# Last down phase of a decoder layer: tokens 0 to 256 as the stationary operand, four weight tiles as the moving one

## What is computed

```python
x = layer_norm(ALPHA * x + merged @ w_out, ln1_g, ln1_b)
f = (jax.nn.silu(x @ w_ff_gate) * (x @ w_ff_up)) @ w_ff_down
x = layer_norm(ALPHA * x + f, ln2_g, ln2_b)
```

## Time and profile before

| | us |
|---|---|
| median of 3 runs | 929.28 (929.07 to 929.48) |
| the profiled execution | 929.93 |
| its span in the trace | 927.1 |

### The profile page before, as it was taken

How to read it: one execution, slowest core, us unless ns; L and a number is a source line. 1 busy time by engine, 2 the same in 40 slices (tenths; PEclk the granted TensorE clock), 3 DMA queues, 4 the chain that set the end, 5 groups by cost and what they waited for, 6 DMA issues and landing times.

```text
span 927.1 us, 18700 instructions
## 1 busy us (share of the span) xinstructions
PE 911.2 (98%) x7211; PEld 906.1 (98%) x7211; DVE 769.3 (83%) x1147; ACT 453.2 (49%) x783; POOL 328.8 (35%) x330
## 2 busy tenths in 40 slices
PE   9999999999999999999999999999999999999995
PEld 8999999999999999999999999999999999999995
DVE  2699999999869888877786699988888888788456
ACT  4422232226666634555543457676546656455432
POOL 4666565758300000000005451455633546321104
PEclk9999999999999999999999999999999999999998
DMA  7733333222436534332334230533443333432412
GB/s 228 200 86 92 89 100 90 71 66 80 139 120 227 183 95 122 97 108 80 107 97 136 70 91 1 138 92 92 121 108 92 92 92 98 129 93 63 133 34 96
DMA packets 169813, 98.49 MB, mean 106 GB/s; under 512 B 5338, under 2 KB 165890, under 8 KB 169745
## 3 DMA queue, kind: packets, MB, share of 16 engines
q1 hardware_dynamic: 167513, 96.66, 35.9%
q10 hardware_dynamic: 2232, 0.92, 0.4%
HBM read 89.94 MB, written 7.62 MB: 105 GB/s over the span
## 4 chain that ended last, share of the span: by engine, by line
PE 89%; DVE 5%; POOL 2%; ACT 2%; issue 1%; DMA 1%; SPq 0%; POOLq 0%; DVEq 0%; ACTq 0%
PE main L1550 38%; PE main L1711 33%; PE aux L1711 5%; PE main L1783 3%; PE aux L1550 3%; PE main L2046 1%; PE aux L1536 1%; PE aux L1963 1%; POOL h_f L886 1%; PE main L1963 1%; DMA raw<-in_w_in 1%; PE main L1586 1%; POOL r_tok L937 1%; POOL r_tok L939 0%; DVE aux L2563 0%
## 5 line engine op out<-in xcount | busy, mean ns | idle before, releaser
L757 POOL TENSOR_TENSOR w_lo<-raw,w_hi 128x1024 fp32r<-128x1024 f32 (+1 forms) x46 | 110.3, 2403 | 343.1 <-ACT w_hi L949 336.2
L1550 PE MATMUL main<-x_hi,w_lo 128*128 128x272 f32 x752 | 156.0, 288 | 0.0
L1550 PE MATMUL main<-x_hi,w_hi 128*128 128x272 f32 x752 | 155.7, 289 | 0.0
L1550 PE MATMUL main<-x_lo,w_hi 128*128 128x272 f32 x752 | 155.2, 288 | 0.0
L949 ACT ACTIVATE w_hi<-raw 128x1024 fp32r<-128x1024 f32 x103 | 108.6, 1057 | 70.3 <-PE main L1550 38.0
L1550 PEld LDWEIGHTS main<-x_lo,w_hi 128*128 128x128 f32 x752 | 118.2, 189 | 0.0
L1550 PEld LDWEIGHTS main<-x_hi,w_lo 128*128 128x128 f32 x752 | 118.1, 188 | 0.0
L1550 PEld LDWEIGHTS main<-x_hi,w_hi 128*128 128x128 f32 x752 | 117.4, 189 | 0.0
L2171 DVE SCALAR_TENSOR_TENSOR aux<-glu_pad,miscT,aux 128x512 f32<-128x512 f32 x112 | 75.1, 747 | 0.0
L894 POOL TENSOR_TENSOR h_lo<-h_f,h_hi 128x272 fp32r<-128x272 f32 x50 | 49.3, 992 | 56.4 <-ACT h_hi L1383 55.5
L1550 PE MATMUL main<-y,w_hi 128*128 128x272 f32 x384 | 63.6, 288 | 0.0
(11 more groups left out here) (467 smaller groups left out, 2927.1 us busy)
## 6 DMA issues: line engine op xcount, KB each, us to landing
raw<-in_w_in SPq DMA_DIRECT2D x63, 512.0 KB, 4.1
raw<-in_w_ff_gate SPq DMA_DIRECT2D x22, 512.0 KB, 4.0
raw<-in_w_ff_up SPq DMA_DIRECT2D x22, 512.0 KB, 5.3
raw<-in_w_branch SPq DMA_DIRECT2D x32, 256.0 KB, 3.5
raw<-in_w_ff_down SPq DMA_DIRECT2D x32, 256.0 KB, 3.9
raw<-in_w_out SPq DMA_DIRECT2D x8, 512.0 KB, 3.9
raw<-in_w_ff_down SPq DMA_DIRECT2D x16, 192.0 KB, 3.4
kept_sums<-g_made_hi SPq DMA_DIRECT2D x4, 544.0 KB, 3.6
```

The source lines that it names most:

```text
L757: pool.tensor_tensor(w_lo[s][:, 0:n, :], raw[s][:, 0:n, :], w_hi[s][:, 0:n, :].bitcast(F32), ALU.subtract).then_inc(w_lo_ready, 1)
L1550: mm = pe.matmul(ps[:, h, :], w[s][:, k, :], x[:, h * HALF:(h + 1) * HALF], start=(first and k == 0 and j == 0), stop=(last and k == n - 1 ...
```

## The change

The eight tiles are done in the order 0, 2, 1, 3, 4, 6, 5, 7, for columns 256 to 544 alone (`item_a`, weights stationary as before, 288 columns moving). Tokens 0 to 256 are done after all of these in four pieces (`item_b`): the hidden rows of 128 tokens are stationary, and four weight tiles, 512 columns, move. Sums come out by rows: partition = token. So all eight weight tiles are kept split until the end (`rows_w`, in the places of `w_hi`, `w_lo`, `x_hi` and `x_lo`). What must still be turned for these tokens is `merged` as it was before the third phase (`turn_b`); ACT copies it to `r_tok` (`rows_b`), DVE adds the sums there (`add_b`) and measures 512 columns at once (`measure_b`). POOL's part of the last norm is reduced to group 3 and to 256 columns of group 1.

```diff
-         + [("ff", q) for q in range(15, KF - 2)] + [("plain", m) for m in range(KD)])
+         + [("ff", q) for q in range(15, KF - 2)] + [("plain", m) for m in (0, 2, 1, 3, 4, 6, 5, 7)])
+TURNS = (("a", 0), ("a", 1), ("a", 2), ("a", 3), ("r", 0), ("a", 4), ("r", 1), ("a", 5), ("r", 2),
+         ("a", 6), ("a", 7), ("r", 3))
...
+            def item_a(i, f):
+
+                for k, (wt, x) in enumerate(plain_weights(S_PLAIN + i, f)):
+                    mm = pe.matmul(a_bank(i), wt, x[:, C_A:NT],
+                                   start=(f == f0 and k == 0), stop=(f == KF - 1 and k == 2))
...
+            def item_b(t, f):
+
+                j, h = divmod(t, 2)
+                k = f // 2 - FIRST_PAIR[2] + f % 2 * PAIRS[2]
+                wh, wl = (rows_w[h][b][:, :, k, :] for b in range(2))
+                xh, xl = (x[:, j * P:j * P + P] for x in hid_row(f))
+                out = b_bank(t).rearrange("p (m n) -> p m n", m=RING)
+                for n, (wt, x) in enumerate(((wl, xh), (wh, xl), (wh, xh))):
+                    mm = pe.matmul(out, x, wt, start=(f == f0 and n == 0), stop=(f == KF - 1 and n == 2))
...
+            def turn_b(t):
...
+                for m in range(RING):
+                    mm = pe.transpose(main[:, 1 + 2 * h, m * P:m * P + P],
+                                      merged[:, RING * h + m, j * P:j * P + P], ident[:, :])
...
+            def add_b(t):
+
+                j, c = t // 2, t % 2 * RING * P
+                rows_ = r_tok[:, j, c:c + RING * P]
+                ve.wait_ge(plain_done, KD + t + 1)
+                ve.wait_ge(rows_out, turned_at("r", t))
+                ve.tensor_tensor(rows_, b_bank(t), rows_, ALU.add).then_inc(plain_out, 1)
+
+            def measure_b(t):
+
+                j, c = t // 2, t % 2 * RING * P
+                ve.wait_ge(plain_out, KD + t + 1)
+                link(ve.bn_stats(bn[:, j, t % 2, :], r_tok[:, j, c:c + RING * P]))
...
-            for n, (j, cols) in enumerate(((3, slice(0, D)), (2, slice(D // 2, D)), (1, slice(D // 2, 3 * D // 4)),
-                                           (1, slice(3 * D // 4, D)))):
+            for n, (j, cols) in enumerate(((3, slice(0, D)), (1, slice(3 * D // 4, D)))):
```

More of the change, by code:

```diff
@@ L1476, in last_rows @@
[L1476 to L1485, removed]
+            left_high(s + 5)
@@ L1957, in plain_weights @@
                 return (wl[:, k, :], xh), (wh[:, k, :], xl), (wh[:, k, :], xh)
[L1959 to L1964, removed]
-                return mm
[L1967 to L1972, removed]
+            f0 = 2 * FIRST_PAIR[2]
@@ L1999, in _ @@
                 for f in range(f0, f0 + 4):
-                    plain(m, f, first=(f == f0))
-                if m == 0:
+                    item_a(i, f)
+                if i == 0:
                     product_4(S_PLAIN - 1)
-            for m in range(2):
+            for i in range(RING):
                 pe.wait_ge(hid_lo_ready, made(lo_order, 2, 2, "a21"))
-                plain(m, f0 + 4)
+                item_a(i, f0 + 4)
                 pe.wait_ge(hid_lo_ready, made(lo_order, 2, 2, "a22"))
-                plain(m, f0 + 5, last=True).then_inc(plain_done, 1)
@@ L2008, in _ @@
-            for m in range(2, WHOLE):
-                pe.wait_ge(left_lo_ready, S_PLAIN + m + 1)
-                pe.wait_ge(plain_out, m - 1)
+                item_a(i, f0 + 5).then_inc(plain_done, 1)
+            for i in range(RING, KD):
+                pe.wait_ge(left_lo_ready, S_PLAIN + i + 1)
+                pe.wait_ge(plain_out, i - 3)
+                for f in range(f0, f0 + 4):
+                    item_a(i, f)
+                if i == 4:
+                    turn_a(0)
+                    turn_a(1)
+                elif i == 5:
+                    turn_a(2)
+                    turn_a(3)
+                    turn_b(0)
+                else:
+                    turn_a(i - 2)
+                    turn_b(i - 5)
+                item_a(i, f0 + 4)
+                item_a(i, f0 + 5).then_inc(plain_done, 1)
@@ L2011, in _ @@
+            pe.wait_ge(plain_out, 5)
+            for f in range(f0, f0 + 4):
+                item_b(0, f)
+            turn_a(6)
+            turn_a(7)
+            turn_b(3)
+            item_b(0, f0 + 4)
+            item_b(0, f0 + 5).then_inc(plain_done, 1)
+            for t in range(1, 4):
+                if t == 3:
+                    pe.wait_ge(rows_out, turned_at("r", 3))
+                else:
+                    pe.wait_ge(plain_out, (6, 8)[t - 1])
                 for f in range(f0, KF):
-                    if f == f0 + 4:
-                        for before in ((0, 1) if m == 2 else (m - 1,)):
-                            turn_rows(before)
@@ L2015, in _ @@
-                    mm = plain(m, f, first=(f == f0), last=(f == KF - 1))
+                    mm = item_b(t, f)
                 mm.then_inc(plain_done, 1)
[L2018 to L2029, removed]
@@ L2049, in _ @@
-            turn_last(len(LAST) - 1)
         @block.vector
@@ L2826, in last_statistics, with measure_a @@
+            def measure_a(i):
+                ve.wait_ge(rows_turned, turned_at("a", i))
+                for j in range(3):
+                    q = P if j < 2 else B * T
+                    ins = ve.bn_stats(bn[0:q, 2 + j, M_ORDER[i], :], aux[0:q, i % 2, j * P:j * P + P])
+                    if j < 2:
                         link(ins)
                 ins.then_inc(rows_measured, 1)
+            def add_b(t):
[4 more added lines that the diff above has]
+                ve.tensor_tensor(rows_, b_bank(t), rows_, ALU.add).then_inc(plain_out, 1)
@@ L2860, in finish @@
                   .then_inc(rows_ready, 1)
-            left, right = slice(0, D // 2), slice(D // 2, D)
+            whole = slice(0, D)
             s = S_PLAIN
@@ L2891, in _ @@
+            measure_a(5)
+            add_a(7)
+            measure_a(6)
+            measure_a(7)
             aggregate(0)
-            add_last(4)
+            ve.wait_ge(bn_var, 1)
+            ve.wait_ge(vecs_copied, 2)
+            ve.wait_ge(rows_out, turned_at("a", 7))
+            weigh(rs_tok[:, :], B * T, NTILE, whole)
             last_scale(0)
-            ve.wait_ge(vecs_copied, 2)
-            ve.wait_ge(rows_out, WHOLE + 4)
-            weigh(rs_tok[:, :], B * T, NTILE, slice(0, D))
@@ L2907, in _ @@
+            finish(r_tok[:, 2, :], P, 2, whole)
+            add_b(1)
+            measure_b(1)
             aggregate(1)
             ve.wait_ge(bn_var, 2)
-            ve.wait_ge(rows_out, WHOLE + 8)
-            weigh(r_tok[:, 0, left], P, 0, left)
+            weigh(r_tok[:, 0, :], P, 0, whole)
             last_scale(1)
-            weigh(r_tok[:, 0, right], P, 0, right)
-            finish(r_tok[:, 0, :], P, 0, slice(0, D))
+            finish(r_tok[:, 0, :], P, 0, whole)
+            add_b(2)
@@ L2914, in _ @@
+            measure_b(2)
+            add_b(3)
+            measure_b(3)
+            aggregate(2)
+            ve.wait_ge(bn_var, 3)
+            left, third = slice(0, D // 2), slice(D // 2, 3 * D // 4)
             weigh(r_tok[:, 1, left], P, 1, left)
-            for cols in (slice(0, D // 4), slice(D // 4, D // 2)):
-                finish(r_tok[:, 1, cols], P, 1, cols)
+            last_scale(2)
+            finish(r_tok[:, 1, left], P, 1, left)
+            weigh(r_tok[:, 1, third], P, 1, third)
@@ L2919 @@
+            finish(r_tok[:, 1, third], P, 1, third)
 N_SMALL = 21
```

265 lines of the change are left out of this document (123 added, 142 removed).

## The result

| | before | changed |
|---|---|---|
| median, us | 929.38 (929.07 to 929.48, 4 runs) | 924.02 (923.39 to 924.67, 4 runs) |
| the profiled execution | 929.93 | 924.05 |
| its span | 927.1 | 922.1 |

The ratio is 0.9941, with a 95% interval of 0.9928 to 0.9953. The change makes the kernel faster by 5.4 us. 3.6 were forecast, so the direction is right, and the time lies at the lower edge of the range (as ratios, 0.9941 against 923.9 / 929.28 = 0.9942).

What follows compares the result with a forecast made beforehand. POOL's share of the last norm was taken to set the old end, DVE's list the new: 903.6 plus 14.4 gives 918.0, the tail 921.4 against 924.84; with overlap 3.6 us gained, 929.28 - 3.6 = 925.7, range 923.9 to 927.3.

Steps and rivals of the forecast that it cites:

- DVE, not PE, sets the new end: Tail of the third phase: DVE's last list, not PE's last sum, bounds the changed kernel; 3.6 us gain, 78%.
- The margin: At the last add: DVE comes to it at 916.3, 1.4 us later than PE's last sum at 914.9.
- is set by POOL's share of the last norm: End of the kernel before: eight POOL operations back to back until 924.84, not the last matmul, set the end.
- the splits and the turns: Third phase: splitting weights and turning items were costed at nothing, being covered by other work.
- the rival of new stalls: First part of the third phase: five turns each wait 0.5, DVE's list starts 2.5 later; gain 1.1, 928.2; 8%.
- The rival in which a measurement's width is free: DVE's last list: 512-column measurements cost 0.28, four save 1.6 us, DVE keeps up; gain 5.2, 924.1; 8%.
- 903.6: Start of DVE's last list, after the eighth turn, six measurements, and ACT's copies including the offset vector.
- 1.7 us: Between the eighth turn and DVE's last list: six DVE measurements of 0.28 each.
- 14.4 less 0.2: DVE's unbroken last list, to group 1's aggregate: 14.4 us of operations, 0.2 taken off for overlap of neighbours.
- Two rivals, at 924.1 and 924.5: DVE keeps up through nearly free measurement width, 924.1, 8%; 512-column matmuls cost no more than 288-column ones, 924.5, 2%.
- The rival in which wide matmuls run faster than one column per cycle: PE's 72 wide matmuls: 0.133 each, 9.6 us in all, PE ends 7.3 earlier; gain 4.8, 924.5; 2%.
- The slower rival: PE's 72 wide matmuls: each costs four 128-column ones, 0.44, 31.7 us in all; 10.2 later, 939.5; 4%.

Runs made afterwards that it cites:

- b_pool_short: Kernel before, with only the changed kernel's shares of the last norm (POOL less, DVE its 768 columns): 930.17 us, ratio 1.0014.
- turns_late: Changed kernel with the seventh and eighth items' turns and the fourth early-row turn six 512-column matmuls later on PE: 925.77 us, ratio 0.9957.
- weigh_early: Changed kernel with the first operation of DVE's last list waiting only for the scale vector's copy, not the offset vector's: 923.77 us, ratio 0.9942.
- again: The changed kernel itself, unaltered, timed once more beside variants as their base: 924.09 us, ratio 0.9944.
- quarters: Changed kernel with each 512-column matmul issued as four of 128 columns, one weight tile each: 938.85 us, ratio 1.0101.

## Why the prediction was right or wrong

**Right: what sets the new end.** "DVE, not PE, sets the new end" holds. The chain runs as forecast, the last add does not wait for PE, three more matmuls cost nothing, and a shift of the eighth turn costs its full length. The margin was 0.75 us and not 1.4.

**Too strong: what ended the kernel before.** That its end "is set by POOL's share of the last norm" held for 0.76 us only: in `b_pool_short` POOL ends 1.37 sooner, and the end moves 0.8 later, since DVE took over. The 3.6 do not rest on this, since they were added up along DVE's new list.

**Right: PE.** Of 0.213 to 0.242 for a 512-column matmul I took 0.235; it is 0.231. The last sum came at 914.11, where 914.9 was forecast: 0.26 of this is an earlier start of the phase, 0.28 lies between that start and the eighth turn, and 0.25 in the 60 matmuls behind the turn, which were taken 0.004 too slow each. Nothing waits in the phase, so the splits and the turns were rightly costed at nothing, and the rival of new stalls falls.

**Right: the new operations.** A measurement of 512 columns takes 0.69 (forecast 0.68, bounds 0.28 to 0.88), an add 0.68, ACT's 256 columns 0.60, POOL's pair 0.72 each; the tail from the aggregate to POOL's end is 3.47 (3.42). The rival in which a measurement's width is free falls.

**Wrong: the size, 3.6 for 5.4.** The step that failed is the start of DVE's last list, "903.6", and in it above all the six measurements, taken as "1.7 us" behind the eighth turn. The list started at 902.48, 1.12 sooner, and `turns_late` (1.38 for 1.38) and `weigh_early` (0.69 for 0.77) show that such a shift reaches the end nearly one for one, as long as PE is not the bound. It divides so:

- The eighth turn ended at 899.76, not 900.3: 0.26 from the phase's earlier start in this profile, and 0.28 from PE's paces.
- The six measurements were charged as "1.7 us" behind that turn, at 0.28 each. They take 1.27 together, 0.21 each, because neighbours that do not wait for one another overlap, and they start at 899.47, since the first three read the seventh item's turns: they were done 0.98 behind the turn, 0.72 less. The overlap was seen in the earlier trace rows (16 in 3.5 us) and used for the list only, not here.
- From the measurements to the list's start, the copies took 1.74 for 1.64, 0.1 more. The other 0.04 is rounding (903.64).

The list itself took 14.02 us (902.48 to 916.50), where 14.4 less 0.2 were forecast: the two aggregates of 12 values take 0.21 each, and I had charged 0.34, the price of one of 48 values; the other operations together took 0.08 more than charged. The last store took 2.13 for 2.3. Together 1.12 + 0.18 - 0.05 + 0.17 = 1.4, which is the difference between the forecast span (921.2 + 2.3 = 923.5) and the measured 922.1.

What is left, 0.4 us of the medians, lies outside the spans. Over the 9 runs of before that stand beside `again`, time less span has a median of 2.34 (1.91 to 2.79); over the runs of `again` it is 1.99 (1.92 to 2.00). Why the changed kernel needs less outside its span was not tried, and stays open.

**The numbers of the faster rivals.** Two rivals, at 924.1 and 924.5, lie nearer to the measured 924.02 than the forecast does. That is chance: a 512-column measurement is not nearly free (0.69), and a 512-column matmul costs 0.231 and not 0.133.

**The pace of a wide matmul.** The rival in which wide matmuls run faster than one column per cycle falls: they are spaced by 0.231, where one column per cycle of 2.4 GHz would be 0.213. The Trainium skill (TensorE: Matmul & The Clock Gate, Back-to-back issue gap) states 131 ns as the sustained spacing of 512-column matmuls. No stretch of them in the traces here comes near it. By the same section's formula for a single matmul the estimate is 216 ns; the measurement is 7% above that.

**The slower rival** did not come about, but its price was real. Four separate matmuls of 128 columns take 4 x 0.112 = 0.45 (forecast 0.44), and `quarters` ended at 938.85, where that rival had 939.5. What the trace of before could not tell is that one instruction over four weight tiles does not pay the price of four.

## What to carry to other kernels

When one engine's last list sets the end, look for its start: every term ahead of that start counts fully, and a group of operations that do not wait for one another is charged by the group's length in the trace, from the moment at which its first member can begin, not as a count times a mean behind its last input. If the chain ends on one engine, ask how far the next one is behind it (0.76 us here) before that engine's work is handed over. A last sum that comes out in the layout of the output takes the turn, and all groups but one, off the tail.

## What the hardware showed that I had not expected

From 256 columns down to 128 a matmul's pace does not fall: 128 columns 0.112, 256 columns 0.113, then 272 at 0.1255 and 288 at 0.133, and 512 at 0.231, all at a granted clock of 1.00 and with a load of the stationary operand in front of each matmul. At 128 columns in place of 256 a product saved nothing; half as wide and twice as many cost twice as much. And the 0.1175 of the kernel before for 256 columns was not the least: the same width, with the weights moving, was paced at 0.113.
